# Expert blocks of 32 rows on four column tiles in a hybrid decoder step on Trainium2

## The reference

```python
def grouped_experts(xf, experts, gates, w_gate, w_up, w_down):
    ...
    def expert_block(args):
        xblk, e = args
        h = jax.nn.silu(xblk @ w_gate[e]) * (xblk @ w_up[e])
        return h @ w_down[e]
    ...
    y = yb[dest] * sg[:, None].astype(yb.dtype)
    return jax.ops.segment_sum(y, st, num_segments=n_tok)
...
    ffn = hier_moe(x, router_group_w, router_group_b, router_expert_w, router_expert_b, w_gate, w_up, w_down)
    x = layer_norm(DN_ALPHA * x + ffn, ln2_g, ln2_b)
```

## Time and profile before

| what | value |
|---|---|
| median of 3 runs | 3031.38 us (3028.86 to 3047.07) |
| profiled execution, first to last instruction (its span; no other time of it was taken) | 3052.3 us |
| from the first product of `up` to the end of the last `down` | 2347.56 to 2959.32 us |
| PE busy over the span | 2768.2 us |

### The profile page before, as it was taken

One profiled execution on the slowest core, in us unless ns is written; L12 is line 12 of the kernel. 1 busy time (PEld: TensorE's weight loads), 2 busy tenths in 40 slices (PEclk: granted clock), 3 DMA queues, 4 the chain that ended last, 5 costly groups with the idle time before them and its releaser, 6 DMA issues. The chain is left out here.

```text
span 3052.3 us, 45862 instructions
## 1 busy us (share of the span) xinstructions
PE 2768.2 (91%) x15004; PEld 1756.4 (58%) x15006; DVE 1848.3 (61%) x2800; ACT 1275.9 (42%) x2356; POOL 774.8 (25%) x1019
## 2 busy tenths in 40 slices
PE   8999999998998988889787978999995999999978
PEld 7887888798996444445455654565453333333323
DVE  2599524699934898778877546644435433343438
ACT  2111222378875686876878655210000111111116
POOL 3344332233331133322334141113300000000016
PEclk9999999999999999999999989999996999999999
DMA  4323332134442212102000277346514778678437
GB/s 139 95 91 94 97 119 74 39 93 127 120 145 95 76 49 73 50 7 65 19 8 15 101 232 271 114 153 213 181 47 178 273 286 312 250 257 299 159 145 289
DMA packets 235832, 416.04 MB, mean 136 GB/s; under 512 B 29372, under 2 KB 153532, under 8 KB 222858
## 3 DMA queue, kind: packets, MB, share of 16 engines
q1 hardware_dynamic: 177938, 270.20, 26.4%
q0 software_dynamic: 25472, 90.08, 8.6%
q10 hardware_dynamic: 32256, 53.58, 4.9%
HBM read 518.11 MB, written 96.91 MB: 201 GB/s over the span
## 5 line engine op out<-in xcount | busy, mean ns | idle before, releaser
L471 PE MATMUL p_ps_acc<-p_x_hi,p_w_hi 128*128 128x352 f32 (+2 forms) x1480 | 528.2, 357 | 12.4 <-POOL p_w_lo L398 10.6
L471 PE MATMUL p_ps_acc<-p_x_lo,p_w_hi 128*128 128x352 f32 (+2 forms) x1480 | 519.2, 351 | 0.0
L471 PE MATMUL p_ps_acc<-p_x_hi,p_w_lo 128*128 128x352 f32 (+2 forms) x1480 | 519.1, 351 | 0.0
L3226 PE MATMUL e_ps_G<-l_wgu,e_xT 128*64 x768 | 343.8, 601 | 24.4 <-DVE g_shared L3343 13.6
L3228 PE MATMUL e_ps_G<-g_shared,e_xT 128*64 128x512 f32 x768 | 343.9, 601 | 0.0
L471 PEld LDWEIGHTS p_ps_acc<-p_x_hi,p_w_hi 128*128 128x128 f32 (+1 forms) x1480 | 276.6, 187 | 66.3 <-issue 19.0
L471 PEld LDWEIGHTS p_ps_acc<-p_x_lo,p_w_hi 128*128 128x128 f32 (+1 forms) x1480 | 276.8, 187 | 27.6 <-issue 0.5
L471 PEld LDWEIGHTS p_ps_acc<-p_x_hi,p_w_lo 128*128 128x128 f32 (+1 forms) x1480 | 276.4, 187 | 27.0
L3226 PEld LDWEIGHTS e_ps_G<-l_wgu,e_xT 128*64 128x64 f32 x768 | 104.1, 138 | 251.4 <-issue 251.4
L396 POOL CAST p_w_hi<-g_late 128x1024 fp32r<-128x1024 f32 x74 | 94.6, 1279 | 587.8 <-PE p_ps_acc L471 443.8
L792 DVE SCALAR_TENSOR_TENSOR g_shared<-g_late,p_taps,g_shared 128x1024 f32<-128x1024 f32 x240 | 227.2, 988 | 4.2
(11 more groups left out here) (594 smaller groups left out, 5209.7 us busy)
## 6 DMA issues: line engine op xcount, KB each, us to landing
l_wgu<-in_w_gate_dram SPq DMA_DIRECT2D x96, 1024.0 KB
l_wgu<-in_w_up_dram SPq DMA_DIRECT2D x96, 1024.0 KB
l_wd<-in_w_down_dram SPq DMA_DIRECT2D x92, 1024.0 KB
g_late<-in_w_in_dram SPq DMA_DIRECT2D x72, 512.0 KB
yb<-e_y SPq DMA_DIRECT2D x48, 512.0 KB
featT<-p_stage ACTq DMA_DIRECT2D x28, 528.0 KB
featT<-p_stage ACTq DMA_DIRECT2D x28, 512.0 KB
g_late<-featT SPq DMA_DIRECT2D x56, 256.0 KB, 3.0
```

The source lines that it names most:

```text
L471: m = nc.tensor.matmul(acc[slot][tb][0:rows, 0:width], wp[:, slot, k, 0:rows], xp[:, k, at], start=(k == 0 and i == 0), stop=(k == KD - 1 ...
L3226: a = nc.tensor.matmul(pG[slot][halves(0), :].rearrange("p (g f) -> p g f", g=2), xT[:, slot, k, halves(0)], w.gu[:, bass.ds(s, 1), :, k, ...
```

## The change

Blocks have 32 rows (HB = P // CT with CT = 4), NHB becomes 161 blocks and NBLK 41 groups of four blocks; on these inputs 144 blocks and 36 groups are filled. In `up` and `down` four blocks stand side by side on 32 columns of PE's array each. Block 0 streams its weights from their slot, blocks 1 to 3 from three sets of copies in `g_shared`, `g_late` and `g_early` (and one own tile): DVE copies two of them, ACT one. PE's order in a group is now `up(j)`, then the two halves of `turn(j + 1)` in turn with the two halves of `turn_hidden(j)`, then `down(j)`; `gated`, `turn_hidden` and the copy of hT go in halves. xT has one buffer instead of two.

Every expert's weights are loaded once, in the order of the experts, without tables: expert e+4 goes to the slot of expert e when the last group with rows of expert e is done (`groups_before`). The first four are loaded when `route` begins. The results are stored by ACT's queue. The residual rows are no longer all loaded before `combine`: one tile in `route`, five after the last `up`, the others in `combine` six tiles ahead. In `route` the tables `weight_slot` and `is_new` are gone, and the table of experts is made in two parts.

```diff
-HB = P // 2
+CT = 4
+HB = P // CT
 NHB = (2 * TT - NE) // HB + NE
-NBLK = (NHB + 1) // 2
+NBLK = (NHB + CT - 1) // CT
...
-EARLY, HELD = 7, 13
+OWN, NEXT = 1, 6
...
+def load_down(q, c, w, e, slot):
+    src = c.inp["w_down"][0].rearrange("e (k p) d -> p e k d", k=2)
+    q.dma_start(w.d[:, bass.ds(slot, 1)], src[:, bass.ds(e, 1)]).then_inc(w.d_loaded[slot], 16)
...
+                def expert(i, slot):
+                    n = sp.value_load(groups_before[0:1, bass.ds(WS * i + slot, 1)], min_val=1, max_val=NBLK)
+                    sp.wait_ge(gu_full, n * CT + CT)
+                    load_gate_up(sp, c, w, WS * i + WS + slot, slot)
+                    down_landed((slot - 1) % WS, i + (1 if slot else 0))
+                    gate_up_landed(slot, i + 1)
+                    sp.wait_ge(y_full, n * 2 * CT + 2 * CT)
+                    load_down(sp, c, w, WS * i + WS + slot, slot)
...
                     for k in range(KD):
+                        for x in range(CT):
+                            if x and k % 2 == 0:
+                                pe.wait_ge(gu_kept[x], CH * j + (k // 2 + 1))
+                            weights = gu_of[x][:, :, k, :] if x else w.gu[:, bass.ds(e % WS, 1), :, k, :].rearrange("p a g f -> p (a g) f")
+                            m = nc.tensor.matmul(pG[slot][tile_of(x), :].rearrange("p (g f) -> p g f", g=2), xT[:, k, tile_of(x)], weights,
+                                                 start=(k == 0), stop=(k == KD - 1))
...
+                def group(i, b, more):
+                    j = 2 * i + b
+                    e = pe.value_load(expert_of[0:1, bass.ds(CT * j, 1)], min_val=0, max_val=NE - 1)
+                    up(b, j, e)
+                    for k in range(2):
+                        if more:
+                            turn(1 - b, i + b, j + 1, k)
+                        turn_hidden(j, k)
+                    down(j, e)
...
             @block.scalar
+                def group(i, b, more):
+                    j = 2 * i + b
+                    if more:
+                        e = last_of(j + 1)
+                    silu(b, j)
+                    if more:
+                        keep_x(j + 1)
+                        copy_gate_up(e)
+                    keep_y(i, b, j)
+                    if more:
+                        copy_down(e)
+                    store(b, j)
...
             @block.vector
+                def group(i, b, more):
+                    j = 2 * i + b
+                    if more:
+                        e = middle_of(j + 1)
+                    for k in range(2):
+                        gated(b, j, k)
+                    for k in range(2):
+                        keep_hidden(j, k)
+                    if more:
+                        copy_gate_up(e)
+                    dve.wait_ge(y_full, 2 * CT * j + 3 * CT)
+                    dve.wait_ge(y_stored[b], 16 * i + 16)
+                    nc.vector.tensor_copy(y[:, b, 0:512], pY[0][:]).then_inc(y_kept[0], 1)
+                    if more:
+                        dve.wait_ge(y_full, 2 * CT * j + 4 * CT)
+                        copy_down(e)
...
                 for t, n in enumerate(rows):
+                    if t + NEXT < NTL:
+                        load_residual(sp, c, last, t + NEXT)
                     sp.wait_ge(biased, t + 1)
```

More of the change, by code:

```diff
@@ L2984, in _ @@
             def _(sp):
[L2985 to L2989 removed]
+                for e in range(WS):
+                    load_gate_up(sp, c, w, e, e)
+                for t in range(OWN):
+                    load_residual(sp, c, last, t)
             @block.gpsimd
@@ L3007, in _ @@
             def _(act):
+                for e in range(WS):
+                    load_down(act, c, w, e, e)
                 act.wait_ge(e_ready, 1)
@@ L3156, in store @@
-                def store(j, slot):
-                    sp.wait_ge(y_kept[0], j + 2)
-                    sp.wait_ge(y_kept[1], j + 2)
-                    sp.dma_start(c.yb[bass.ds(j * P, P), :], y[:, slot, :]).then_inc(y_stored[slot], 16)
-                gate_up(2, 0)
-                for t in range(EARLY, HELD):
-                    sp.dma_start(last.z[t], c.x1[t * P:t * P + P, :]).then_inc(last.loaded, 16)
-                with sp.Fori(0, NBLK // 2 - 2) as i:
-                    for x in range(2):
-                        gate_up(2 * i + x + 3, 2 - 2 * x)
-                        down(2 * i + x + 2, 2 * x)
-                        store(2 * i + x, x)
@@ new lines, in _ @@
+                for slot in range(WS):
+                    gate_up_landed(slot, 0)
+                    if slot:
+                        down_landed(slot - 1, 0)
+                with sp.Fori(0, NE // WS - 1) as i:
+                    for slot in range(WS):
+                        expert(i, slot)
+                down_landed(WS - 1, NE // WS - 1)
+                sp.wait_ge(x_turned, 2 * NBLK)
+                sp.dma_start(w.rows[:, 0, :], c.inp["ln2_g"].to_broadcast([P, D])).then_inc(w.affine_loaded, 16)
@@ L3188, in _ @@
+                sp.dma_start(w.rows[:, 1, :], c.inp["ln2_b"].to_broadcast([P, D])).then_inc(w.affine_loaded, 16)
+                sp.wait_ge(gu_full, CT * NBLK + CT)
+                for t in range(OWN, NEXT):
+                    load_residual(sp, c, last, t)
             @block.gpsimd
@@ L3214, in up, with turn @@
-                def up(slot, j, s, turn):
-                    pe.wait_ge(x_kept, 2 * j + 4)
-                    for x in range(2):
-                        pe.wait_ge(w.gu_loaded[2 * slot + x], 32 * turn + 32)
-                    pe.wait_ge(h_done, j + 1)
+                pe.sem_inc(gu_full, CT)
+                pe.sem_inc(y_full, 2 * CT)
+                def turn(slot, turns, j, h, first=False):
+                    pe.wait_ge(w.x_loaded[slot], 16 * turns + 16)
+                    if not first:
+                        pe.wait_ge(x_kept, 2 * j - 2 + (h + 1))
+                    for k in range(4):
+                        m = nc.tensor.transpose(pX[h][:, part(k)], xg[:, slot, 4 * h + k:D:KD], c.ident[:])
+                    m.then_inc(x_turned, 1)
@@ L3259, in slots @@
-                def slots(j):
-                    return pe.value_load(weight_slot[0:1, bass.ds(2 * j, 1)], min_val=0, max_val=WS - 1)
-                def group(i, last):
-                    s = [slots(2 * i + b) for b in range(2 if last else 3)]
-                    for b in range(2):
-                        j = 2 * i + b
-                        if b + 1 < len(s):
-                            up(1 - b, j + 1, s[b + 1], i + b)
-                        turn_hidden(j)
-                        if not last:
-                            turn(i + 1, b, j + 2)
-                        down(b, j, s[b], i)
@@ new lines, in group @@
+                def group(i, b, more):
[7 more added lines that the diff above has]
+                    down(j, e)
+                for h in range(2):
+                    turn(0, 0, 0, h, first=True)
@@ L3382 @@
+                e = middle_of(0)
+                copy_gate_up(e)
+                copy_down(e)
+                with dve.Fori(0, rounds) as i:
+                    for b in range(2):
+                        group(i, b, True)
+                for j in range(2 * rounds, NBLK):
+                    group(j // 2, j % 2, j + 1 < NBLK)
 ZS = 3
```

372 lines of the change are left out of this document (153 added, 219 removed).

## The result

The changed kernel takes 3001.69 us, the median of four runs (2998.55 to 3007.42), beside 3033.11 us for the kernel before in four runs of the same comparison: a ratio of 0.9892, interval 0.9867 to 0.9918. The forecast was 2964. The time lies inside the range, but less than half of the forecast gain is there. The profiled execution has a span of 2998.3 us, 54.0 less than before.

What follows compares the result with a forecast made beforehand. PE's stream in the experts' stage was taken as the bound, padding groups included. Terms: groups -74.8, weights +2, route 0, combine +4, last store +1, sum -67.8 us; 3031.4 becomes 2963.6 us, range 2945 to 3004.

Steps and rivals of the forecast that it cites:

- late weights: Experts' stage: today's 19 us of waiting for weights nearly gone, +2 us put on, bounds 0 and 20.
- longer small hops of the chain: Between `up` and `down`: small hops estimated from neighbouring rows, giving the chain bounds of 2.5 and 3.6 us.
- Fewer groups on four full tiles: `up` and `down`: 41 groups instead of 48, a pass of four blocks still taking 0.429 us.
- The rivals of the lossy pass: `up` and `down`: four streams disturb each other; up to 0.47 us a pass, chance 0.05; beyond it, 0.08.
- The chain between `up` and `down`: From the start of the last `up` pass to the first `down` product: 2.86 us, against 2.09 before.
- The clock rival: PE falls to half clock in the new gap of each group: 41 x 1.7 = +70 us, 3034 us; chance 0.05.
- A group: Experts' stage: one group takes 13.1 us, bounds 12.7 and 13.9; 41 of them 537 us, -74.8 us.
- the loop turn and the table value: Between groups: 0.3 us in the mean for a new loop turn and the table value PE's queue reads.
- Copies and weights: Experts' stage: DVE's 9.7 and ACT's 9.0 us of work hidden within 13.1 us a group; late weights +2 us.
- Route: `route`: small operations saved against the first `up` waiting for ACT's copies, sum 0.
- Combine and the last store: `combine`: 11 residual tiles loaded inside it, +4 us, bounds 0 and 13.7; last group's store behind five tiles, +1.
- its distance of 20.9 us from the median: Whole kernel: the median lies 20.9 us below the profiled span, and the same difference was taken for the changed kernel.

Runs made afterwards that it cites:

- e1_silu_first: The changed kernel with one single-column SiLU on ACT ahead of its loop: 2979.06 us, ratio 0.9776 to the kernel before.
- e3_pause: e1_silu_first plus an idle ACT copy ahead of SiLU in the first group of each loop turn and the group behind the loop: 3023.09 us.
- the second pair of profiles: The kernel before and the changed kernel, each run and profiled again without edits: medians 3049.45 and 3018.57 us.
- e5_one_row: e1_silu_first with only one row loaded of each of the 11 residual tiles in `combine`: 2968.03 us.
- e2_small_residual: The changed kernel with only 16 of 128 rows loaded of each of the 11 residual tiles in `combine`: 3012.72 us.
- e9_after_store: e1_silu_first with twelve residual tiles before `combine`, five after the last `up` and seven once the last results' store landed: 2973.43 us.

## Why the prediction was wrong in size

The direction and the mechanism of the gain were right, the price of the open chain was not. The forecast of -67.8 us compares with -42.0 once the chance part ahead of `route` is left out; the terms below add up to it. That the median lies inside the range is partly luck: its upper part was meant for lossy passes, late weights and longer small hops of the chain, and what filled it, the table load and its pauses, is in none of them.

*Fewer groups on four full tiles: right.* A pass is 0.429 us, to the digit. The rivals of the lossy pass do not hold here: 16 passes of four tiles take what 16 passes of two took. Nor does the figure that the Trainium skill gives (TensorE: Matmul & The Clock Gate, Measured speedup vs the span model), 2.38x for three column tiles of 32 with 512 columns, by which a pass would be 0.54 us as an estimate.

*The chain between `up` and `down`: the step that failed.* The sum of hops was good where no load stands in it: from the start of the last `up` pass to the first `down` 2.82 us (2358.58 to 2361.40 in the profile after) against 2.86. But its first hop, "SiLU starts after 0.74 us", was read from a group whose table was in place, and the one load of the kernel before was not weighed: the sum has it at nothing, without a reason. In 20 groups the hop has 1.28 us more. That is 25.7 us, shown by e1_silu_first. Before, the load came once, at 2347.3 us, ahead of the first product of `up`. What it would have cost there in each turn, with SiLU beside the `down` of another group, wasn't tried. The Trainium skill (ScalarE: Activation LUTs, What ACT_TABLE_LOAD costs) gives 1283 ns for the load and some 1380 ns of drain with it for every switch. The trace agrees with the first number. Of the second it shows nothing: a group with a load is 13.99 - 12.71 = 1.28 us longer.

*The clock rival: right in kind, with a wrong condition and size.* I priced it at 1.7 us in all 41 groups with a chance of 0.05, for a pause of 1.1 us. The pause is 0.52 us in the groups without a load, since the transposes of x lie in two halves around the hidden ones, and there the clock holds. It also stands elsewhere than I said: before the hidden transpose, ended by `gated` (L3337), and not before `down`. Where the load makes it 1.8 us, it fell in 8 of 20, for 11.4 us (the difference of the stage in e1_silu_first, less its loads). That the pause alone does it, e3_pause shows.

*A group: 13.1 forecast, 12.71 measured.* The 0.3 us of the loop turn and the table value and the 0.1 of more semaphores are not there: the next `up` starts 0.43 us after the last `down` pass, as within one product. With 523.0 for the stage without loads, against 537, this is -14.0 us, the largest miss in the other direction.

*Copies and weights: right, the latter by more than forecast.* Nothing in `up` waits for them, though ACT's four pieces take 3.89 us and w_down's 1.90. The +2 us for late weights were 0, so -2.

*Route: 0 forecast, +0.85 measured* (+2.5 in the second pair of profiles).

*Combine and the last store: +5 forecast, +8.9 measured*, within 0 to 13.7 for `combine` (+11.4 in the second pair). The DMA time of the residual tiles was sized well: 12.6 us go with them in e5_one_row, against 13.7. That the middle is full at 419 GB/s was right too. What was wrong is how much of it the six tiles of lead would hide: with 9.7 us of tail gone in e5_one_row, most of it is on the path.

The sum again: -67.8 - 14.0 + 25.7 + 11.4 - 2 + 0.85 + 3.9 = -42.0 to the rounding, and -51.8 + 8.9 + 0.85 = -42.0. The median moved by less, 31.4 us in the first comparison and 35.0 in the last; the profile of before was the slower of its two in the stage by 3.3 us, and taking its distance of 20.9 us from the median over to the other kernel did not hold: the span of the changed kernel's profile lies 3.4 us under its median.

Left open: why every second or third of the pauses of 1.6 to 1.8 us lowers the clock and the others don't; why the gathers' packets are slower in e2_small_residual; and SiLU in halves, which would shorten the chain, wasn't tried.

## What to carry to other kernels

When a change moves an ACT function, look for ACT_TABLE_LOAD rows in the trace of before and ask with which table each loop is then entered: a load that stood once ahead of a loop can come back in every turn, and one tiny activation ahead of the loop takes it out. When a chain is laid open between two bursts of PE, price its pause twice, as time and as a possible half clock after it. And before transfers are moved into a stage, look not at its mean but at its fullest windows, and find an emptier place for them, such as the wait for the last results.

## What the runs showed of the hardware that was not expected

- An ACT_TABLE_LOAD took 1.283 us each time, also when it loaded the same table again and again in a loop, and added 1.28 us to its group, beside what the clock cost after some of them.
- PE's granted clock fell to 1.2 GHz in 8 of 20 groups after pauses of 1.8 us, in a stage that is otherwise busy and granted 0.98, and in 10 of 21 after pauses of 1.6 us (2.1 the last of them), at regular distances of 54.6 or 81.9 us but for the last; the earlier trace rows had shown a pause of 1.94 us with no effect. After pauses of 0.5 us it never did (41 groups of e1_silu_first).
- Four column tiles with four different moving operands of 512 f32 columns ran at the pace of two, 0.429 us a pass, while DVE was busy 355 and ACT 332 of 560 us.
- In the tail the gathers' packets of 4096 bytes took 181 ns in the mean in the kernel before, 175 in the changed one, 191 in e2_small_residual and 161 in e9_after_store, while those of the loads and stores took 163 or 164 in all four.
